# Page numbers read ahead of slot waits, and the last two tiles of a projection moved behind the scores of the first two heads

## The reference

```python
def odd_mixer(h, pos0, k_past, v_past, s_re, s_im, P, o):
    z = h @ P['od_w_in'][o]
    q, k, v, u = _split(z, [dC, dC, dC, dD])          # 512 columns each: 16 tiles of 128, u is tiles 12 to 15
    q = rmsnorm(q.reshape(B, L, H_C, HD_C), P['moba_gq'][o])
    k = rmsnorm(k.reshape(B, L, H_C, HD_C), P['moba_gk'][o])
    k_all = jnp.concatenate([k_past.astype(k.dtype), k], axis=1)
    v_all = jnp.concatenate([v_past.astype(v.dtype), v], axis=1)
    o_c = moba_attend(q, k_all, v_all, pos0, P['rel_bias'])
    y, hr, hi = s5_scan(u..., s_re, s_im, ...)
    ...
# k_past, v_past of the 8 samples: 8 pages each of 128 tokens, picked by page_table from a pool
k_past = cache_moba_k[:, page_table].reshape(N_ODD, Bs, past, H_C, HD_C)
```

## Time and profile before

| | |
|---|---|
| time, three runs | 1025.82, 1030.28, 1031.37 us (median 1030.28) |
| profiled execution | 1033.7 us, of it 1031.9 us span |
| busy share of the span | PE 95%, PEld 85%, DVE 70%, ACT 41%, POOL 10% |
| mean granted clock of PE | 0.967 |
| data | 183.75 MB read, 7.35 MB written, 185 GB/s over the span |
| the chain that ended last, by engine | PE 77%, issue 9%, DVE 6%, SP's queue 3%, ACT 2%, DMA 2% |

### The profile page before, as it was taken

One profiled execution on the slowest core, in us unless ns is written; L12 is line 12 of the kernel. 1 busy time (PEld: TensorE's weight loads), 2 busy tenths in 40 slices (PEclk: granted clock), 3 DMA queues, 4 the chain that ended last, 5 costly groups with the idle time before them and its releaser, 6 DMA issues.

```text
span 1031.9 us, 21037 instructions
## 1 busy us (share of the span) xinstructions
PE 984.3 (95%) x8388; PEld 873.2 (85%) x8388; DVE 718.8 (70%) x1548; ACT 427.1 (41%) x813; POOL 98.5 (10%) x201
## 2 busy tenths in 40 slices
PE   7998999989999999999999996898999999999996
PEld 5876988878987999999997763477899799999996
DVE  5876648876756789887647585685375579998642
ACT  3453226725565443444422112622366554434320
POOL 0010021100100112212000000001000012121200
PEclk9988999979999999999999997989999999999998
DMA  8331023613694555565456888974844454555531
GB/s 345 134 129 42 4 84 128 231 62 123 227 344 164 172 182 186 172 233 186 155 184 209 300 276 287 319 251 175 339 164 162 196 179 165 192 177 206 220 113 43
DMA packets 41571, 192.46 MB, mean 187 GB/s; under 512 B 4602, under 2 KB 5754, under 8 KB 24578
## 3 DMA queue, kind: packets, MB, share of 16 engines
q1 hardware_dynamic: 35858, 165.30, 45.9%
q0 software_dynamic: 4576, 24.25, 6.1%
q10 hardware_dynamic: 1040, 1.57, 0.4%
HBM read 183.75 MB, written 7.35 MB: 185 GB/s over the span
## 4 chain that ended last, share of the span: by engine, by line
PE 77%; issue 9%; DVE 6%; SPq 3%; ACT 2%; DMA 2%; POOL 1%; DVEq 0%; ACTq 0%; POOLq 0%
PE bank L1378 76%; DVE work L2132 2%; SPq L692 2%; DVE work L2135 1%; PE bank L1381 1%; ACT work L844 1%; SPq L665 1%; POOL work_r L793 1%; DMA ring<-in_pool_v 1%; DMA ring<-in_od_in 1%; DVE work L3049 1%; DMA x<-in_x 0%; DVE sq L2132 0%; ACT lnb L844 0%; ACT hr L844 0%
## 5 line engine op out<-in xcount | busy, mean ns | idle before, releaser
L1378 PE MATMUL bank<-h_r,ring_r 128*128 128x264 f32 (+1 forms) x896 | 237.7, 286 | 0.2 <-DVE ring_r L2132 0.2
L844 ACT ACTIVATE work_r<-ring 128x2048 fp32r<-128x2048 f32 (+1 forms) x60 | 125.0, 2087 | 198.8 <-PE bank L1378 198.8
L1378 PE MATMUL bank<-h_r,work_r 128*128 128x264 f32 x704 | 200.7, 285 | 0.0
L1378 PE MATMUL bank<-sq_r,work_r 128*128 128x264 f32 x704 | 199.8, 284 | 0.0
L2132 DVE TENSOR_TENSOR ring_r<-ring,work_r 128x2048 fp32r<-128x2048 f32 (+1 forms) x60 | 151.3, 2525 | 42.5 <-ACT work_r L844 42.5
L1378 PE MATMUL bank<-h,ring 128*128 128x264 f32 x720 | 172.1, 396 | 1.0 <-DMA ring<-in_od_in 1.0
L1378 PEld LDWEIGHTS bank<-h_r,ring_r 128*128 128x128 f32 x896 | 162.6, 188 | 0.8 <-issue 0.6
L1378 PEld LDWEIGHTS bank<-h,ring 128*128 128x128 f32 x720 | 138.9, 195 | 28.0 <-issue 3.7
L1378 PE MATMUL bank<-work_r,ring_r 128*128 128x264 f32 (+1 forms) x480 | 135.9, 283 | 0.0
L1378 PEld LDWEIGHTS bank<-h_r,work_r 128*128 128x128 f32 x704 | 132.3, 188 | 1.1 <-issue 0.9
L1378 PEld LDWEIGHTS bank<-sq_r,work_r 128*128 128x128 f32 x704 | 132.5, 188 | 0.1
(11 more groups left out here) (283 smaller groups left out, 1339.1 us busy)
## 6 DMA issues: line engine op xcount, KB each, us to landing
ring<-in_gu SPq DMA_DIRECT2D x44, 1024.0 KB, 4.9
ring<-in_down SPq DMA_DIRECT2D x16, 1408.0 KB, 6.0
ring<-in_pool_k SPq DMA_DIRECT2D x64, 256.0 KB, 3.6
ring<-in_pool_v SPq DMA_DIRECT2D x64, 256.0 KB, 4.2
ring<-in_ev_in_a SPq DMA_DIRECT2D x8, 1024.0 KB, 6.7
ring<-in_ev_in_b SPq DMA_DIRECT2D x8, 1024.0 KB, 4.9
work<-in_cv POOLq DMA_DIRECT2D x8, 1024.0 KB, 15.6
ring<-in_od_in SPq DMA_DIRECT2D x8, 1024.0 KB, 4.9
```

What stands on the lines that cost most here:

```text
L844: return nc.scalar.activation(out, in_, func, **k)
L1378: return nc.tensor.matmul(out, lhsT, rhs, start=start, stop=stop, skip_group_check=True)
```

## The change

Two edits. `READ_AHEAD` moves the loads of page numbers: those of slots 10 and 11 go in front of the wait for `pk` 8, those of 12 to 15 together in front of the wait for `pk` 12, and the numbers of 12 to 15 are kept for the values; for the values, 8 and 9 are read in front of `pv` 4, and 10 and 11 in front of `pv` 8. And the tiles 14 and 15 of the input projection leave their place behind kp3: 14 now stands behind the scores of heads 0 and 1, 15 behind `self`, and kp4 behind 15. DVE takes their results out behind its own score work of the first pair.

```diff
+READ_AHEAD = {("pk", 8): (10, 11), ("pk", 12): (12, 13, 14, 15), ("pv", 4): (8, 9), ("pv", 8): (10, 11)}
...
-    lin("od_in", 16, 2, 2048, after=inputs)
+    lin("od_in", 14, 2, 2048, after=inputs)
     order.extend([("vt", 0), ("vt", 1)])
 
     def pages(i):
 
         if i == 0:
+            lin("od_in", 15, 2, 2048, 14)
             order.append(("self",))
+            lin("od_in", 16, 2, 2048, 15)
+            key_pages(4)
...
                 if kind == "page":
-                    numbers = kept[i] if i < KEPT else page_numbers(i)
+                    for n in READ_AHEAD.get((name, i), ()):
+                        later[n] = page_numbers(n)
+                    numbers = kept[i] if i < 8 or (name == "pk" and i < KEPT) else later[i]
                 if s >= SLOTS:
                     last = slots[s - SLOTS][4]
...
-            for m in range(16):
+            for m in range(14):
                 lin("od_in", m, KC, 2, h, T, hready(norms.index(("mix", 1))))
...
                 if i == 0:
-
+                    lin("od_in", 14, KC, 2, h, T)
                     b = begin(("self",))
...
                     end(ins)
+                    lin("od_in", 15, KC, 2, h, T)
+                    key_pages(4)
...
                     for i in pair:
                         scores(i)
+                    if j == 0:
+                        od_in(14)
                     for i in pair:
                         normalise(i)
...
                 if i == 1:
+                    od_in(15)
                     sample_states()
...
             score_rows(1)
-            od_in(14)
             s5_output_matrices(1)
-            od_in(15)
```

More of the change, by code:

```diff
@@ L659, in _ @@
             early = CON["neg"]
-            kept = []
+            kept, later = [], {}
             def page_numbers(i):
```

## The result

The changed kernel takes 1040.84 us (median of four runs, 1040.73 to 1043.83); four runs of the kernel before have a median of 1030.82 us. The ratio is 1.0108, with a 95% interval of 1.0075 to 1.014: about 10 us slower. The profiled execution of the changed kernel took 1040.73 us, 1038.9 of it span.

What follows compares the result with a forecast made beforehand. PE waits for pages that SP issues late, slowed by page-number loads. A held tile 15 and sixteen loads make kp6 13.2 us late; 3.7 come back, so 1030.3 + 9.5 = 1039.8 us, range 1032.5 to 1045.

Steps and rivals of the forecast that it cites:

- The hold: PE ahead of the scores of heads 0 and 1: a new 4.6 us wait for ACT's copies of `vt`.
- PE isn't held: Rival, chance 0.12: copies of `vt` come at once, tile 15 ends at 609.7; +4.2 us, 1034.5 us.
- The slow restart: PE from the first scores to tile 15's end: starts at the lower clock after idling, costing 1.7 us.
- SP ahead of `pk` 11, and the sixteen loads: SP stands before `pk` 11 from 602.3 to 615.0, issues it, then reads sixteen numbers in 8.8 us.
- Landing, kp6, vp0, vp2: Two slots' pages land in 9.0 us; kp6 comes 13.2 us late, vp0 and vp2 9.5 us late.
- the forecast path: From SP's late page issues through page landings to kp6, vp0 and vp2, then DVE's wait; 9.5 us late.
- the tie at vp2: At vp2, the pages of `pv` 4 and 5 land by 661.2, just when PE gets there.
- The sum: 9.5 us late at vp0 and vp2, on into the scans: 1030.3 + 9.5 = 1039.8 us.
- second rival: DMA, not SP, sets the pages' pace: vp0 only 0.7 us late, 1031 us; chance 0.06.
- SP's time doesn't count: Rival, chance 0.06: DMA sets the pages' pace, so the sixteen loads are made up; 1031 us.
- Faster: the reads leave the chain: Rival, chance 0.06: pages come early, vp0's 4.66 us wait and 1.7 us slow start go; 1023.9 us.
- Worse: delays add up: Rival, chance 0.10: landings of 11 us, or loads for 8 and 9 delaying vp2; +14, 1044 us.

Runs made afterwards that it cites:

- the kernel with the copies first: The changed kernel with ACT's two copies of `vt` put ahead of the second page score's exponentials; 1037.53 us, ratio 1.0053.
- the second profile: The changed kernel, unchanged, profiled once more beside a repeat of the kernel before; 1043.55 us, against 1029.89 for before.

## Why the prediction was right, step by step

**The hold.** Forecast 4.6 us, released by ACT; measured 4.51 and 4.02. That it carries weight is shown by the kernel with the copies first, which loses the hold and 4.0 us of the stretch. The rival "PE isn't held" put its own price at 4.2 us; made real, it came to 5.1 us in the stretch and 6.9 in the time.

**The slow restart.** Forecast 12.15 us from the scores to the end of tile 15, with 1.7 us for the clock; the chain has 11.89. The scores and tile 14 took 1.75 and 4.86 us, 1.8 more than the 1.14 and 3.68 at the higher clock. The size came true, the reason given for it is weak: the idle time alone doesn't say which restart is slow. In the earlier trace rows kp5 is slow behind 1.19 us and kp7 fast behind 1.68, and the hold of 4.6 us is not longer than the 4.66 ahead of vp0.

**SP ahead of `pk` 11, and the sixteen loads.** Forecast a wait of 12.7 us and loads of 8.8 us; measured 11.7, and 8.95 from the first load (619.20) to the next issue (628.15), where the loads are 0.55 us apart. The Trainium skill (DMA: Bandwidth & Descriptors, section Latency and other measured facts) gives some 600 ns as the floor of such a load; this case's rows lie below it, at 0.27 us for a load alone and 0.55 from one load to the next.

**Landing, kp6, vp0, vp2.** From the first issue of `pk` 12 to kp6 it was 637.03 - 628.15 = 8.9 us (forecast 9.0). kp6, vp0 and vp2 were forecast for 634.9, 647.5 and 661.2. In the second profile, where kp3 starts within 0.4 us of where it did before, they start at 634.89, 647.92 and 661.59; in the first, less the 2.5 us that were there ahead of kp3, at 634.5, 647.4 and 660.3. In the first profile the forecast path is there: vp0 waits 4.01 us for a page DMA, and the tie at vp2 is a DMA wait of 0.81 us. In the second it isn't: vp0 waits 3.07 us for ACT, and vp2 for no page. There the chain runs from kp6 through the scores of heads 2 and 3 to DVE and ACT, a path that the prediction doesn't name. The two paths come out within about a microsecond of each other, so that the second profile fits so well at vp0 and vp2 is in part luck.

**The sum.** Forecast +9.5 us at the scores of heads 6 and 7; measured +9.1 (first profiles) and +10.3 (second ones). The median came out at 1040.84 us for 1039.8.

**What it had not seen.** Two things more, neither of which moved the sum. It names no wait ahead of kp5, where 4.04 us stand; in the change kp6 is later still and swallows it, but without loads it is part of what remains. By the prediction's terms the moved tiles without the loads would make vp0 0.7 us late, the figure that it gives for its second rival; with no loads in the stretch vp0 came 47.5 us behind kp3 instead of 42.75, 4.8 us late. And it told the story as one chain in which the loads lie behind the slot; the table shows that they are partly alternatives: taking out the hold alone (4.0 us) or moving the loads alone (3.1 us) gives back less than half of the 9.1 us, and both together 9.0.

**The rivals.** "SP's time doesn't count" falls: without the loads the kernel before is 0.9919 [0.989, 0.9947] of itself, and 7.8 us of the stretch go. The Trainium skill (the same page, section Issuing engines are not separate DMA queues) calls the sequencer's time to start a DMA usually small beside the DMA; in this case, with an address to be loaded for each DMA, it wasn't: 4.3 us for a slot, where two slots landed in 8.9. "Faster: the reads leave the chain" named 1023.9 us and a condition, that tile 15 frees its slot early enough; with the tiles left alone and three slots' loads in waits that were there anyway, 1025.04 us were measured. (Of the six slots that it counts only four are sped up by the change, since `pv` 0 and 1 use kept numbers before too; its price doesn't hang on this.) "Worse: delays add up" didn't happen: from the first issue of `pk` 12 to kp6 it was 8.9 us, and 9.4 in the second profile.

## What to carry to other kernels

Before an in-order engine's work is moved behind something that waits, list who waits for the moved work: here two tiles that PE could well do later held a buffer, the buffer held a queue, and the queue held every page behind it. Reads that a queue needs go into waits that it already has, no more of them than each wait is long; sixteen in a row behind a wait are a new wait. And if two delays share a path, try them in all combinations, since each alone looks cheap while the other is there. A mend that brings the old time back has not shown that the change is free: compare it with the old kernel under a like mend (61.7 against 54.4 us here).

## What the hardware showed that was not expected

The same instructions, from the scores of heads 6 and 7 to the end of the scans, took 61.56 us in two executions and 58.19 and 56.97 us in two others, one of each kernel in either group; the granted clock was 0.89 in the first two and 0.97 in the others. This is 3 to 5 us, as much as many an edit is worth, and it doesn't follow the kernel. A difference of two single profiles can be off by that much. Over all twelve profiles kp3 starts anywhere from 592.96 to 597.76 us, and from the scores of heads 6 and 7 to the end it takes 370.4 to 375.2, which is why the stretch, from one event to another on the same path, was compared here rather than two spans.
